# Raw fp32 gate chunks, most of them inside the expert phase, and fp32 gathers for the first three experts

## What is computed

```python
h   = LN1(alpha*h + a)
gi, gp = top-1 of softmax(h @ w_rg + b_rg)                 # 4 groups
ei, ew = top-2 of (h @ w_re + b_re)[gi], softmax * gp      # 8 experts in the group
m   = sum over the two experts e of ew * ((silu(h @ w_eg[e]) * (h @ w_eu[e])) @ w_ed[e])
pe  = (p @ w_ple_proj) * sigmoid(h @ w_ple_gate)           # w_ple_gate: 1024 x 1024
h   = LN2(alpha*h + m + pe)
```

## Time and profile before

| what | value |
|---|---|
| median of 3 runs | 920.84 us (918.92 to 921.12) |
| profiled execution: its own time | 921.15 us |
| its span (first to last instruction) | 919.0 us |
| PE busy | 853.7 us (93%) |
| weight loads (PEld) busy | 546.4 us (59%) |
| DVE / ACT busy | 423.7 (46%) / 264.5 (29%) |
| DMA | 266.68 MB, 290 GB/s on average |
| raw_x chunks | 192 of 1 MB, 24.1 us from issue to landing |
| raw_dense chunks | 45 of 1 MB, 4.9 us from issue to landing |

### The profile page before, as it was taken

One profiled execution on the slowest core, in us unless ns is written; L12 is line 12 of the kernel. 1 busy time (PEld: TensorE's weight loads), 2 busy tenths in 40 slices (PEclk: granted clock), 3 DMA queues, 4 the chain that ended last, 5 costly groups with the idle time before them and its releaser, 6 DMA issues.

```text
span 919.0 us, 16481 instructions
## 1 busy us (share of the span) xinstructions
PE 853.7 (93%) x6596; PEld 546.4 (59%) x6596; DVE 423.7 (46%) x783; ACT 264.5 (29%) x363; POOL 49.5 (5%) x89
## 2 busy tenths in 40 slices
PE   8999999999999999899999999989898989898984
PEld 5997777889998897665444444434343434343421
DVE  6588999989976468864311110101010101010127
ACT  5354234454228633433111111111111111111111
POOL 1200000000000000000000000000000000000000
PEclk9999999999999999999999999999999999999998
DMA  8844233143343435836999999999999999999981
GB/s 318 282 143 143 94 138 135 46 141 135 138 152 106 170 138 205 345 138 264 414 419 422 421 422 422 422 421 421 422 423 422 422 422 422 421 423 421 422 315 59
DMA packets 40516, 266.68 MB, mean 290 GB/s; under 512 B 6214, under 2 KB 6486, under 8 KB 9632
## 3 DMA queue, kind: packets, MB, share of 16 engines
q1 hardware_dynamic: 36064, 255.32, 69.4%
q0 software_dynamic: 4416, 10.86, 3.6%
HBM read 258.40 MB, written 13.09 MB: 295 GB/s over the span
## 4 chain that ended last, share of the span: by engine, by line
PE 56%; DMA 32%; DVE 6%; ACT 3%; issue 2%; SPq 1%; ACTq 0%; DVEq 0%
DMA raw_x<-wstream 31%; PE ps L1602 12%; PE ps L1277 7%; PE ps L1279 7%; PE ps L1278 7%; PE ps L1613 4%; PE ps L1316 2%; PE ps L1573 2%; PE ps L1298 2%; PE ps L1317 2%; PE ps L1318 2%; ACT w_hi L474 1%; PE ps L1383 1%; DVE w_lo L724 1%; PE ps L1326 1%
## 5 line engine op out<-in xcount | busy, mean ns | idle before, releaser
L1602 PE MATMUL ps<-raw_x,xs 128*64 128x512 f32 x1024 | 233.6, 596 | 35.3 <-DMA raw_x<-wstream 34.1
L1602 PEld LDWEIGHTS ps<-raw_x,xs 128*64 128x64 f32 x1024 | 79.7, 136 | 160.5 <-issue 158.4
L1613 PE MATMUL ps<-raw_x,actT 128*64 128x512 f32 x512 | 118.3, 599 | 0.0
L1203 DVE COPY actT<-ps 128x256 f32<-128x256 f32 x32 | 13.6, 425 | 224.7 <-PE ps L1620 224.7
L724 DVE TENSOR_TENSOR w_lo<-raw_dense,w_hi 128x2048 fp32r<-128x2048 f32 x44 | 101.8, 2314 | 27.6 <-ACT w_hi L474 27.5
L474 ACT ACTIVATE w_hi<-raw_dense 128x2048 fp32r<-128x2048 f32 x44 | 83.9, 1908 | 79.8 <-PE ps L1298 44.6
L857 DVE SCALAR_TENSOR_TENSOR cT_sb<-uT_sb,conv_par,cT_sb 128x350 f32<-128x350 f32 x210 | 106.6, 575 | 0.6
L1277 PE MATMUL ps<-hT_hi,w_hi 128*128 128x320 f32 x304 | 95.6, 314 | 0.2 <-issue 0.2
L1279 PE MATMUL ps<-hT_hi,w_lo 128*128 128x320 f32 x304 | 93.9, 309 | 0.0
L1278 PE MATMUL ps<-hT_lo,w_hi 128*128 128x320 f32 x304 | 93.9, 309 | 0.0
L1209 DVE SCALAR_TENSOR_TENSOR act_rows<-gate_silu,slot_weight,ps 64x512 f32<-64x512 f32 x32 | 23.6, 739 | 139.4 <-ACT gate_silu L663 139.4
(11 more groups left out here) (294 smaller groups left out, 1042.0 us busy)
## 6 DMA issues: line engine op xcount, KB each, us to landing
raw_x<-wstream SPq DMA_DIRECT2D x192, 1024.0 KB, 24.1
raw_dense<-wstream SPq DMA_DIRECT2D x45, 1024.0 KB, 4.9
y_rows<-rows_sb POOLq DMA_DIRECT2D x10, 256.0 KB, 8.8
ln_gb<-ln POOLq DMA_DIRECT2D x2, 1024.0 KB, 7.4
y_gathered<-y_rows SPq DMA_DIRECT2D x4, 512.0 KB, 5.4
const<-consts SPq DMA_DIRECT2D x1, 1310.5 KB, 12.4
rows_sb<-x SPq DMA_DIRECT2D x2, 512.0 KB, 3.8
ln_gb<-ln_in POOLq DMA_DIRECT2D x1, 1024.0 KB, 5.2
```

Source lines behind the costliest of these rows:

```text
L1602: m = mm(ps[rows_at, 1, :], xs[:, 4 * half + k, :], w[i][:, k, :], start=half == 0 and k == 0, stop=half == 1 and k == 3)
L1613: m = mm(ps[64 * b:64 * b + 64, 4, :], aT[:, 2 * half + k, :], w[:, k, FF * b:FF * b + FF], start=half == 0 and k == 0, stop=half == 1 and ...
```

## The change

- Chunks 41 to 44: only chunk 41, gate (0,0), stays ahead of the experts, after the fold and before the ranks. It is used as raw fp32, without hi and lo. The other three go one at a time to a buffer of their own, `raw_gate`, and PE uses them as raw fp32 after the pairs of experts 3, 7 and 11 (`late_gate_chunk`, `GATE_AT`), that is after experts 8, 16 and 24. SP fetches the first of them right behind the first fill of the ring, the second after refill group 5, the third after group 9, each of these two behind a wait on `gate_pe`. Sigmoids and `gates(b)` move behind the chunks that they need.
- The transposed h is kept once, in fp32: `h1_low`, the `w_route` split and POOL's addition `h1T_last_tile` go. The logits are one fp32 product per contraction block, alternating between column halves 0 and 64; `logT` is written by two copies, and the fold adds the halves.
- The gathers of experts 0, 1 and 2 are fp32: `gather_f32`, 24 matmuls of `rows_sb` x `onehot_f32`, the third tile with its 64 rows. The bf16 parts of token tiles 1 and 2 are made in the course of the first experts; PE waits for them before expert 2 is run.
- The first six expert chunks are issued after chunk 41 of the dense ring instead of after chunk 43; the other six on `pe_done`.

The core of the diff:

```diff
+EARLY = GATE0 + 1
+GATE_AT = (4, 8, 12)
...
-        with sp.Fori(1, 11) as n:
+        with sp.Fori(1, 10) as n:
...
+        for i in range(GATE0 - 1, EARLY):
+            sp.wait_ge(ss("pe_done"), i - RAW_D + 1)
+            sp.dma_start(raw_d[:, i % RAW_D, :], wstream[i]).then_inc(raw_d_in[i % RAW_D], 16)
...
+        for l in range(6):
             fetch(0, l)
-        sp.wait_ge(ss("pe_done"), DENSE - RAW_D)
...
+        for done, l in ((39, 8), (40, 9), (40, 10), (41, 6), (41, 11), (EARLY, 7)):
+            sp.wait_ge(ss("pe_done"), done)
             fetch(0, l)
+        fetch_gate(EARLY)
...
-        refill_from(0)
+        with sp.Fori(1, GATE_AT[0] + 2) as g:
+            refill(0, g)
+        sp.wait_ge(ss("gate_pe"), 1)
+        fetch_gate(EARLY + 1)
+        with sp.Fori(GATE_AT[0] + 2, GATE_AT[1] + 2) as g:
+            refill(0, g)
+        sp.wait_ge(ss("gate_pe"), 2)
+        fetch_gate(EARLY + 2)
...
-                go(logT[:], ps[0:72, 3, 0:TOK], ACT.Identity, bias=b_route[:]).then_inc(ss("logT_ready"), 1)
+        go(logT[0:36, :], ps[0:36, 3, 0:TOK], ACT.Identity, bias=b_route[0:36, :]).then_inc(ss("logT_ready"), 1)
+        go(logT[64:100, :], ps[64:100, 3, 0:TOK], ACT.Copy).then_inc(ss("logT_ready"), 1)
...
+        def pick_f32(e):
+
+            if e:
+                dve.wait_ge(ss("x_gathered"), e)
+            tt(onehot32[:], iota[:].unsqueeze(1).broadcast_to([128, TILES, SLOTS]),
+               rankm[:, :, e:e + 1].broadcast_to([128, TILES, SLOTS]), ALU.is_equal).then_inc(ss("onehot32_ready"), 1)
...
         for k in range(KT):
-            w = w_route_r[:, k, :, :].rearrange("p a c -> p (a c)")
-            mm(ps[0:72, 3, 0:TOK], w, h1T[0][:, k, :], start=k == 0, stop=False)
-            m = mm(ps[0:72, 3, 0:TOK], w, h1T[1][:, k, :], start=False, stop=k == KT - 1)
+            c = 64 * (k % 2)
+            m = mm(ps[c:c + 36, 3, 0:TOK], w_route[:, k, :], h1T[:, k, :], start=k < 2, stop=k >= KT - 2)
...
+        def gate_chunk(w, half):
+
+            w = w.rearrange("p (k c) -> p k c", k=4)
+            for t in (2, 0, 1):
+                for k in range(4):
+                    if t == 2:
+                        m = last_tile(GATE_BANKS[t], h1T[:, 4 * half + k, 256:TOK], w[:, k, :], half == 0 and k == 0, half == 1 and k == 3)
+                    else:
+                        m = mm(ps[:, GATE_BANKS[t], :], h1T[:, 4 * half + k, 128 * t:128 * t + 128], w[:, k, :],
+                               start=half == 0 and k == 0, stop=half == 1 and k == 3)
...
+        def late_gate_chunk(n):
+
+            pe.wait_ge(ss("raw_gate_in"), 16 * n + 16)
...
+            gate_chunk(raw_g[:], (n + 1) % 2).then_inc(ss("gate_pe"), 1)
...
+        def gather_f32(e):
+
+            pe.wait_ge(ss("onehot32_ready"), e + 1)
+            for k in range(KT):
+                for t in range(TILES):
+                    m = mm(ps[:, 7, SLOTS * k:SLOTS * k + SLOTS], rows[0:ROWS[t], t, 128 * k:128 * k + 128], onehot32[0:ROWS[t], t, :],
+                           start=t == 0, stop=t == TILES - 1)
...
-        gate_chunk(0, 1)
-        gate_chunk(1, 0)
-        gate_chunk(1, 1)
-        pe.wait_ge(ss("part_last"), TILES)
-        gather(0, 0, late=True)
+        gather_f32(0)
```

More of the change, by code:

```diff
@@ L685, in rounds @@
         def rounds(r):
-            if isinstance(r, int):
-                gate_sigmoids(0)
+            first = isinstance(r, int)
             x_copy(r * EXPERTS)
-            if isinstance(r, int):
-                gate_sigmoids(1)
+            if first:
+                mid_part(1)
             gate_silu(r * EXPERTS, chunk_of(r, 0, 4))
             x_copy(r * EXPERTS + 1)
+            if first:
+                last_part(1)
+                mid_part(2)
+                last_part(2)
             expert(r, 0, 1, first=True)
             expert(r, 0, 2)
-            with act.Fori(1, PAIRS - 1) as p:
-                for k in (1, 2):
-                    expert(r, p, k)
+            for begin, end, b in ((1, GATE_AT[0], 0), (GATE_AT[0], GATE_AT[2], 1), (GATE_AT[2], PAIRS - 1, None)) if first else ((1, PAIRS - 1, None),):
+                with act.Fori(begin, end) as p:
+                    for k in (1, 2):
+                        expert(r, p, k)
+                if b is not None:
+                    gate_sigmoids(b)
             expert(r, PAIRS - 1, 1, last=True)
@@ L1232, in rounds @@
                 pick(r, 0)
-            else:
-                gates(0)
+            first = isinstance(r, int)
+            if first:
                 slot_values()
             next_pick(r, 1)
-            if isinstance(r, int):
-                gates(1)
+            if first:
+                rest(1)
             glu(r * EXPERTS)
+            if first:
+                rest_2(1)
+                rest(2)
+                rest_2(2)
             next_pick(r, 2)
@@ L1242, in rounds @@
                 expert(r, 0, k)
-            with dve.Fori(1, PAIRS - 1) as p:
-                for k in (1, 2):
-                    expert(r, p, k)
+            for begin, end, b in ((1, GATE_AT[0], 0), (GATE_AT[0], GATE_AT[2], 1), (GATE_AT[2], PAIRS - 1, None)) if first else ((1, PAIRS - 1, None),):
+                with dve.Fori(begin, end) as p:
+                    for k in (1, 2):
+                        expert(r, p, k)
+                if b is not None:
+                    gates(b)
+                if b == 1:
+                    alpha_h1()
             aT_copy(r * EXPERTS + EXPERTS - 2)
@@ L1565, in _, with gather @@
         m.then_inc(ss("rank_psum"), 1)
-        def gather(r, e, late=False):
+        def gather_f32(e):
+            pe.wait_ge(ss("onehot32_ready"), e + 1)
+            for k in range(KT):
+                for t in range(TILES):
+                    m = mm(ps[:, 7, SLOTS * k:SLOTS * k + SLOTS], rows[0:ROWS[t], t, 128 * k:128 * k + 128], onehot32[0:ROWS[t], t, :],
+                           start=t == 0, stop=t == TILES - 1)
+            m.then_inc(ss("x_gathered"), 1)
+        def gather(r, e):
+            if isinstance(r, int) and isinstance(e, int) and e < EXACT:
+                gather_f32(e)
+                pe.wait_ge(ss("onehot_ready"), e + 1)
+                slot_columns(e)
+                return
             pe.wait_ge(ss("onehot_ready"), r * (EXPERTS + 1) + e + 1)
@@ L1575, in gather @@
             m.then_inc(ss("x_gathered"), 1)
-            if not late:
-                slot_columns(e)
+            slot_columns(e)
         def slot_columns(e):
@@ L1646, in rounds @@
                 pe.wait_ge(ss("values_ready"), 1)
-                pe.wait_ge(ss("gate_sig_s"), 4)
+                pe.wait_ge(ss("onehot_ready"), 1)
                 slot_columns(0)
             gate_up(r, 0, 2, 1)
+            gather(r, 1)
+            expert(r, 0, 1)
             if first:
-                pe.wait_ge(ss("gate_sig_s"), 8)
-            gather(r, 1)
-            for k in (1, 2):
-                expert(r, 0, k)
-            with pe.Fori(1, PAIRS - 1) as p:
+                pe.wait_ge(ss("part_last"), TILES)
+            expert(r, 0, 2)
+            if first:
+                begin = 1
+                for n, end in enumerate(GATE_AT):
+                    with pe.Fori(begin, end) as p:
+                        for k in (1, 2):
+                            expert(r, p, k)
+                    late_gate_chunk(n)
+                    begin = end
+            with pe.Fori(GATE_AT[2] if first else 1, PAIRS - 1) as p:
                 for k in (1, 2):
```

165 lines of the change are left out of this document (68 added, 97 removed).

## The result

The changed kernel takes 932.0 us (median of 4 runs, 930.73 to 932.97); the kernel before, measured beside it, 920.1. The ratio is 1.0129, interval 1.0110 to 1.0148: 12 us slower, where 916.5 had been forecast. The profiled execution took 932.97 us with a span of 930.8, 11.8 more than the span before.

A forecast was written before the change was run, and what follows sets the result against it. The saturated expert-weight DMA queue sets the end: first freed buffer, chunks times 2.547 us, idle time, unchanged tail. Terms -18.2 + 8.9 + 5.0 = -4.3 us gave 916.5 against the median; range 907 to 926.

The forecast's parts named there:

- steps 1 to 4: Path from logits through fold, one gate chunk and ranks: first gather at 397.5 instead of 421.19, 23.7 us earlier.
- step 5: First fp32 gather on PE: 5.3 us of overlapping weight loads plus 2.3 for 16 row-shape changes, 7.6 us.
- step 6: Gathers 1 and 2 in fp32 delay freed buffers: queue idles 5.3 and 3.3 us, with the rest +8.9 us.
- step 7: Late gate chunks: two fetches in the saturated stream cost +5.0 us; 3 x 9 us of PE work stays hidden.
- Steps 3 and 4: One raw fp32 gate chunk, 9.0 us on PE, then ranks and one-hot: gather at 397.5 instead of 421.19.
- step 2: Logits and fold: two logT copies no longer stand behind the h1b copy; fold 1.6 us earlier, at 386.15.
- steps 1 and 2: Without the h1T_lo subtraction logits come 1.1 us earlier; with shorter logT copying the fold comes 1.6 us earlier.
- Rival E: PE's clock falls in or after the gathers: 1.7 us lost three times, +5.1, about 921.5; chance 0.15.
- Rival D: fp32 weight loads in the gathers don't overlap: 11.4 us per gather, +7.1 us, about 928; chance 0.15.
- The sum's steepness: Each us of gather time counts three times, before T and in both pauses; nothing is left at 9.0 us.

## Why the prediction was wrong

| term | forecast | measured |
|---|---|---|
| logits, fold, gate chunk, ranks: first gather at (steps 1 to 4) | 397.5 | 396.78 |
| first gather (step 5) | 7.6 us | 12.58 us |
| gate_up of expert 0 begins | 405.9 | 410.04 |
| first buffer freed | 409.6 | 416.1 |
| time lost by the queue in and beside the pauses (step 6) | 8.9 us | 17.1 us |
| two fetches in the saturated stream (step 7) | 5.0 us | 3.3 us by the medians, 5.6 by the traces |
| late gate chunks on PE (step 7) | hidden | hidden |

Steps 3 and 4 were right: the gate chunk 8.95 us for 9.0, and from the start of the fold to the gather 11.2 us for 11.35, where it was 33.5 before. So was the wait for `logT` in step 2, 1.08 us for 1.1. That the gather came 24.4 us earlier for 23.7 is partly luck: among the traces with the same code up to the gather the fold begins anywhere from 383.87 to 387.62 us (385.54 here), so one execution can't show the 1.6 us that steps 1 and 2 promised. Step 7 was right: no pause of the queue near the late gates, with the 60 us windows around them at 1.01.

The step that failed is step 5, "I take 5.3 + 2.3 = 7.6 us", which is a price at full clock and was used as the price. At full clock it was about right (7.1 by the windows). But the clock didn't stay full: it fell to 0.50 in each of the three gathers, and what followed ran at 0.50 too. So the gathers took 12.58, 9.19 and 9.09 us. The signs that the prediction named for being wrong, a gather of over 9 us and a clock row below 1.00 after 397, both came. In numbers against the forecast: the first freed buffer comes 6.5 us later (gather +5.0, gate_up +2.4, less 0.9 gained before and behind the gather), and the pauses cost 8.2 more, from gathers of 9.19 and 9.09 us and a gate_up of 6.56; with 1.4 in the tail that is 16.1, the distance between -4.3 and +11.8. The tail, which the prediction left alone, is not a constant: from the end of expert 31's down to the end of the span it takes 32.6 to 35.4 us in the eleven traces.

Rival E named this mechanism and priced it at 921.5, "no change". Its direction was right and its size wrong: it took 3.4 us at half rate each time, from the recovery in the earlier trace rows, where the first loss lasted from 398 to 415, nearly the whole gather and most of the gate_up. Against 7.1 us for a gather, 3.65 for a gate_up and 3.6 for a down at full clock, the three losses cost 7.9, 5.0 and 3.7 us, 16.6 where E had 5.1. Put into the sum, with 7.1 in place of 7.6 three times, that is -4.3 - 1.5 + 16.6 = +10.8, an estimate from these rows; +11.8 was measured. The row that was held against it, transposes with PE busy 4.21 of 6 us at 1.00, has long dummies between the transposes and no change of row shape inside a group; it was no evidence for a gather. Rival D came nearest to the measured time (928), and by luck: its mechanism is excluded by the padded run, in which loads of 0.19 us each start 0.116 us apart, so they do overlap.

The sum's steepness was right and is what made the error large: the price of a gather counts three times. With 5.57 in place of 7.6 the same sum gives 921.15 - 4.3 - 6.1 = 910.8, and the padded execution that kept its clock took 909.0, with a fold that began 1.6 us earlier than in the changed kernel's trace.

## What to carry to other kernels

A change of the row shape between neighbouring matmuls (128 to 64 rows and back) had two prices here: about 0.1 us each where loads set the pace, and, with 8 or 16 of them in a gather, PE's clock, in the gather and in what follows. Pad the short tile with zeros or run all short tiles together; neither makes the clock certain, so look at it in more than one execution. When work leaves the path ahead of a saturated stream, price what is put in its place at both clock levels, and fill PE's wait for it. And where one queue is full to the end, the time is when it starts, how much it carries and how often it stops; the chain of waits may well name another engine.

## What was not expected of the hardware

- Padding a tile from 64 to 128 rows with zeros made a gather shorter, 5.57 us instead of 9 to 12.6, and the kernel 16 us faster.
- The clock fell without any idle time of PE: in the second and third gather PE was busy 4.00 of 4.00 and 5.00 of 5.00 us when it went from 1.00 to 0.50. The Trainium skill ("TensorE: Matmul & The Clock Gate", Part 1) says that activity releases a throttled clock. Here windows with PE busy throughout stand at either level, so the busy time of a row doesn't tell which.
- Between executions of one kernel the clock may or may not fall: the padded kernel ran from 909.0 to 919.5 us in ten runs, with a mean clock from 0.993 to 0.983, where the kernel before stayed within 918.2 to 923.1 in all of its runs. A few executions of such a kernel tell little.
